# A two-direction delta-rule scan: outputs formed between the steps of its state, products emptied over two banks at once

## The chip, the cores and the metric

One core of a Trainium2 chip runs the whole kernel, a program of two transformer blocks. The metric is the time of one execution on the device in microseconds, the median of several runs. The change touches one function, a scan that runs four times.

## The reference

The part that matters is the RWKV-7 mixer of the first block, for eight heads of 64 columns, 512 tokens of the sequence (the latents) behind 256 tokens of context, forward and backward:

```
def rwkv7_scan(r, w, k, v, a, b, s0):
    def step(S, inp):
        r_t, w_t, k_t, v_t, a_t, b_t = inp
        sa = jnp.einsum('bhvk,bhk->bhv', S, a_t)
        S = S * w_t[:, :, None, :] + sa[..., None] * b_t[:, :, None, :] + v_t[..., None] * k_t[:, :, None, :]
        return S, jnp.einsum('bhvk,bhk->bhv', S, r_t)
    xs = tuple(jnp.moveaxis(t, 1, 0) for t in (r, w, k, v, a, b))
    S_fin, ys = lax.scan(step, s0, xs)
```

The context's final state is the latents' first one, and of the context no output is wanted. The outputs of both directions then go through a norm per head, a bonus and gates. Nothing of this is changed by the edit.

## The kernel before

`rwkv_scan` (from L1479) runs once for each pair of heads (`hp` 0 to 3). Head 0 of the pair stands on partitions 0 to 63, head 1 on 64 to 127. The 768 tokens are cut into `NB` = 12 chunks of `CH` = 64, of which the last `NL` = 8 are latents and the first `NBC` = 4 are context; the two directions `d` go through them in the orders of `order`.

The recurrence is brought into chunk form by a list of jobs, `pe_jobs`, each done for both directions. A job is one 64x64 product per chunk and head, 24 matmuls of fp32 data. The profile records each of these matmuls as two, so 48 records for one direction and 96 for both (L1583 in the helper `product`, L1588 in `turn`). SB, SM, SK and SR are the products of keys, decays and queries; KT, BT, AT and V turn inputs by the identity; T, M and N with their numbers are the rounds that invert the triangular system (solving rounds); XA, XV, ZA, ZV, YA and YV apply the inverse to the keys' side (A) and the values' side (V); G and H are the transition and the input of each chunk's state; RP is the state's factor in the latents' outputs. The jobs differ in how the matmuls lie on the array of 128x128: `four_tiles` goes round all four quarters of it, `both_heads` uses the two on the diagonal, one for each head.

Each job's result takes a region of PSUM of two banks, of which there are three; `region` gives them in turn. Half of the chunks lie in the first bank and half in the second, so that VectorE or ScalarE empties a region with two operations of 128x384 (G with four of 64x384), one after the other; the second one signals. `bank_free` makes a job of TensorE wait until the job three turns before it has been emptied. VectorE has the jobs of `dve_jobs` (masks, sums, L1772 to L1815), ScalarE those of `act_jobs` (copies, L1861), GpSimd multiplies by masks (L1905). ScalarE copies XV and ZV. Between these jobs each engine also does a share of the next pair's preparation (`prep`: among it `scale_rows` with L1310 and L1312, `carries` with L1319 to L1323, and `norm_keys`, L1296) and of the norm and gates of the pair before (`out`: `centre` L1390, `squares` L1376, `variance` L1396, `root` L1381 to L1384, `gates` L1370, `finish` L1406 to L1416). The order is written out by hand. `prep` is there for the first three scans, `out` for the last three.

Then come the ten steps of the state, S1 to S10: for each direction one matmul of a 128x128 by a 128x64 tile (L1700), and on VectorE one operation (L1815) that scales it and adds the chunk's input, giving the next state; S0 (L1780) is a copy. A step of a direction waits for VectorE's operation of the step before. All states are kept, one per chunk. Into the steps 1 to 4 and 7 to 10 TensorE puts a share of the modulation's products (`mods.rows_of`, L1443), from panels of 1 MB that stream in; they collect in a second bank of one region. When they are complete, ScalarE copies their rows (`keep`, L1452, four copies) into a part of the buffer of the outputs, and TensorE turns them into columns (`transpose`, L1460), which VectorE adds to a bias.

The outputs of the latents, job Y, come last: 16 cells for each direction, each the sum of three matmuls (L1706 values' part, L1707 direct part, L1708 state's part), 96 records per direction. Both directions are done in the order Y of direction 0, the modulation's transposes, Y of direction 1. ScalarE copies them out with two operations of 128x256 per direction (L1855). Then all engines meet (L1505), and after every second scan semaphores are cleared and they meet again (L3361).

Of the kernel before, what the change touches and what calls it, by code (L numbers as in the profile page):

```python
# [18 lines left out]
F32 = mybir.dt.float32  # L19
# [1459 lines left out]
def rwkv_scan(nc, g, hp, f, tri, prep_of, out_of):  # L1479
# [22 lines left out]
    dve_jobs = ["SB", "SM", "SK", "SR", "M1", "N1", "M2", "N2", "M3", "N3", "N4", "YA", "YV", "G", "H", "RP"] + ["S0"] + states  # L1502
    act_jobs = ["KT", "M0", "BT", "AKV", "T1", "T2", "T3", "T4", "AT", "XA", "XV", "ZA", "ZV", "Y"]

    with ExitStack() as tmp, nc.Block() as block:  # L1505
# [19 lines left out]
        bank = [[tmp.enter_context(nc.psum_tensor(f"{nm}q{r}{b}", [P, T], F32)) for b in range(2)] for r in range(3)]  # L1525
# [5 lines left out]
        turns += [(job, d) for job in pe_jobs[5:] for d in range(2)]  # L1531
        region = {turn: i % 3 for i, turn in enumerate(turns)}
        mods = ModPanels(nc, g, hp, f.Y[0:66, 1].rearrange("r (n c) -> r n c", c=P), bank[region["S1", 1]][1], prep_banks)
# [3 lines left out]
        cell = lambda d, name, h, i, n: bank[region[name, d]][i // n][head(h), (i % n) * CH:(i % n + 1) * CH]  # L1537
# [5 lines left out]
        halves = [slice(0, NB // 2), slice(NB // 2, NB)]  # L1543
        half_lat = [slice(0, NL // 2), slice(NL // 2, NL)]
# [31 lines left out]
        def _(pe):  # L1576
# [26 lines left out]
            def run(name, d):  # L1603
# [67 lines left out]
                elif name == "ZV":  # L1671
                    act(d, "XV")
# [4 lines left out]
                elif name == "YV":  # L1677
                    act(d, "ZV")
# [14 lines left out]
                elif name[0] == "S":  # L1693
                    n = int(name[1:])
                    dve(d, "H")
                    dve(d, f"S{n - 1}")
                    s = order[d][n]
                    if n == 1:
                        pe.wait_ge(zeroed, 2 + 2 * d)
                    last = mm(bank[region[name, d]][0][:, 0:HD], GT[d][:, s].rearrange("p h t -> p (h t)"), S[d][:, s], start=True, stop=True)  # L1700
# [8 lines left out]
                last.then_inc(pe_done[d], 1)  # L1709
# [13 lines left out]
            for job in pe_jobs[5:]:  # L1723
# [8 lines left out]
                if job == "Y":  # L1732
                    run(job, 0)
                    if out:
                        pe.wait_ge(out.step.sem, 7)
                    elif prep:
                        pe.wait_ge(prep.bonus_kept, 1)
                    mods.transpose(pe)
                    run(job, 1)
# [5 lines left out]
                elif out and job == "ZA":  # L1745
# [3 lines left out]
                elif job in states[0:4]:  # L1749
                    n = states.index(job)  # L1750
                    mods.rows_of(pe, 4 * n, 4 * n + 4)
                elif job in states[-4:]:
                    n = states[-4:].index(job) + 4
                    mods.rows_of(pe, 4 * n, 4 * n + 4)
# [8 lines left out]
        def _(dve):  # L1763
            V = nc.vector
            mask = lambda i, d, n: tri[:, i, d].unsqueeze(1).to_broadcast([P, n, CH])

            def run(name, d):
                own = lambda job: dve.wait_ge(dve_done[d], dve_jobs.index(job) + 1)
                if name == "SM":
                    dve.wait_ge(pe_done[d], pe_jobs.index(name) + 1)  # L1770
                    for b, c in enumerate(halves):
                        step.mark(V.tensor_tensor(MT[d][:, c], part(d, name, b), mask(2, d, NB // 2), ALU.mult))  # L1772
                    step.settle(dve)
                    two = tri[:, 8, 0].unsqueeze(1).to_broadcast([P, NB, CH])
                    V.tensor_tensor(MT[d], MT[d], two, ALU.add).then_inc(dve_done[d], 1)
# [7 lines left out]
                if name in ("SB", "SK"):  # L1783
                    for b, c in enumerate(halves):
                        last = V.tensor_tensor((AT if name == "SB" else AK)[d][:, c], part(d, name, b), mask(0, d, NB // 2), ALU.mult)  # L1785
                elif name == "SR":
                    for b, dst in enumerate((RB, RK)):
                        last = V.tensor_tensor(dst[d][:], part(d, name, b, NL), mask(1, d, NL), ALU.mult)
                elif name[0] in "MN":
# [3 lines left out]
                    for b, c in enumerate(halves):  # L1793
                        last = V.tensor_tensor(buf[d][:, c], buf[d][:, c], part(d, name, b), ALU.add)
                elif name in ("YA", "YV"):
                    buf = XA if name == "YA" else XV
                    for b, c in enumerate(halves):
                        last = V.tensor_tensor(buf[d][:, c], buf[d][:, c], part(d, name, b), ALU.add)
                elif name == "G":
                    two = tri[:, 8, 0].unsqueeze(1).to_broadcast([P, NB // 2, CH])  # L1800
                    for b, c in enumerate(halves):
                        for h in range(2):
                            last = V.tensor_tensor(GT[d][head(h), c, h], part(d, name, b)[head(h)], two[head(h)], ALU.add)
# [1860 lines left out]
```

## Time and profile before

| | us |
|---|---|
| median of 3 runs | 3119.36 |
| the three runs | 3119.67, 3111.02, 3119.36 |
| the profiled execution's own time | 3112.85 |
| its span, from first to last instruction | 3111.1 |
| TensorE busy | 2800.3 (90%) |
| VectorE, ScalarE, GpSimd busy | 1140.3, 939.6, 785.9 |
| mean granted clock of TensorE | 0.962 |
| the four scans begin with the products of SB | at about 408, 523, 642 and 758 |
| all four scans with their ends | 408 to 872 |

Times of rows are counted from the start of the span. "Busy" of TensorE is the union of its matmuls, whose ends are modelled. Idle time stands with the work after it, with what released it; "issue" is idle time in which the engine waited for nothing that the profile shows. The granted clock is a share of 2.4 GHz. The queue q8 carries instructions, not data.

### The profile page before, as it was taken

To read this page: it belongs to the slowest core of one execution; us is meant where nothing else is said; L and a number is where in the kernel's file an instruction comes from. 1 tells how busy PE (TensorE), PEld (TensorE's weight loads), DVE (VectorE), ACT (ScalarE), POOL (GpSimd) and SP (SyncE) were. 2 spreads that over 40 slices of the span, in tenths; PEclk is the share of its full clock that TensorE was granted. 3 is DMA by queue.
4 is the path that set the end of the run, shared out by engine and by line. 5 is a ranking of instruction groups with operands and counts; after the bars stand their busy time and mean duration, and the time that the engine had idled before them with its cause. 6 is when DMAs were issued, how large, how long until landed. Compare 5 with 4: busy or idle time off the path is not lost. (4 is left out here: it accounts for less than half of the span.)

```text
span 3111.1 us, 56253 instructions
## 1 busy us (share of the span) xinstructions
PE 2800.3 (90%) x25293; PEld 2160.5 (69%) x25293; DVE 1140.3 (37%) x1684; ACT 939.6 (30%) x1594; POOL 785.9 (25%) x218
## 2 busy tenths in 40 slices
PE   6987988888866988989899999988999999899998
PEld 4765877777754432333589989986888778678887
DVE  3434765665446000101454546463111113321111
ACT  3123233433322110110344555553222222132222
POOL 3320421231120000000132223221444434334442
PEclk8998999999987999999999999998999999999999
DMA  7111201012031899999422221321233322222221
GB/s 255 55 31 38 68 17 60 11 52 100 6 115 54 347 426 427 427 427 427 148 85 69 68 71 66 82 82 55 82 99 103 96 68 95 81 79 97 95 95 54
DMA packets 171635, 397.69 MB, mean 128 GB/s; under 512 B 9551, under 2 KB 99636, under 8 KB 146036
## 3 DMA queue, kind: packets, MB, share of 16 engines
q1 hardware_dynamic: 170416, 390.70, 34.3%
q8 instruction: 200, 3.28, 0.4%
q10 hardware_dynamic: 980, 3.40, 0.3%
q14 instruction: 39, 0.32, 0.0%
HBM read 387.71 MB, written 4.19 MB: 126 GB/s over the span
## 5 line engine op out<-in xcount | busy, mean ns | idle before, releaser
L179 POOL TENSOR_TENSOR weight_ring_lo<-weight_ring,weight_hi 128x2048 fp32r<-128x2048 f32 (+1 forms) x144 | 657.9, 4570 | 1986.9 <-ACT weight_hi L168 1947.7
L168 ACT CAST weight_hi<-weight_ring 128x2048 fp32r<-128x2048 f32 (+1 forms) x144 | 271.0, 1884 | 670.8 <-PE mlp_o L213 247.7
L213 PE MATMUL a_o<-weight_hi,latT_hi 128*128 128x512 f32 x576 | 176.7, 429 | 2.5 <-PEq L3361 2.5
L213 PE MATMUL a_o<-weight_ring_lo,latT_hi 128*128 128x512 f32 x576 | 158.2, 397 | 0.0
L213 PE MATMUL a_o<-weight_hi,latT_lo 128*128 128x512 f32 x576 | 157.8, 396 | 0.0
L1905 POOL TENSOR_TENSOR rws_E<-rws_AT,rw_tri 128x768 f32<-128x768 f32 x40 | 83.3, 2104 | 287.8 <-DVE rws_AT L1785 186.9
L213 PE MATMUL mlp_o<-weight_hi,mlp_hid_hi 128*128 128x512 f32 x512 | 138.8, 393 | 9.8 <-issue 9.8
L3237 DVE TENSOR_TENSOR x<-x,mlp_o 128x512 f32<-128x512 f32 x64 | 44.0, 687 | 281.4 <-PE mlp_o L213 281.4
L213 PEld LDWEIGHTS a_o<-weight_hi,latT_hi 128*128 128x128 f32 x576 | 132.9, 273 | 16.8 <-issue 8.2
L3222 DVE TENSOR_TENSOR mlp_hid<-mlp_hid,mlp_h 128x512 f32<-128x512 f32 x64 | 41.2, 685 | 272.7 <-ACT mlp_hid L3197 272.7
L213 PEld LDWEIGHTS a_o<-weight_ring_lo,latT_hi 128*128 128x128 f32 x576 | 134.2, 270 | 8.1
L213 PEld LDWEIGHTS a_o<-weight_hi,latT_lo 128*128 128x128 f32 x576 | 134.2, 270 | 7.9
L213 PE MATMUL mlp_o<-weight_ring_lo,mlp_hid_hi 128*128 128x512 f32 x512 | 138.4, 393 | 0.0
L213 PE MATMUL mlp_o<-weight_hi,mlp_hid_lo 128*128 128x512 f32 x512 | 137.1, 390 | 0.0
L204 PE MATMUL mlp_h<-latT_hi,weight_hi 128*128 128x512 f32 x512 | 129.3, 396 | 4.8 <-PEq L3361 4.8
L2441 ACT ACTIVATE moe_silu<-moe_t 128x256 f32<-128x256 f32 x32 | 12.3, 384 | 388.2 <-PE moe_t L2400 387.4
L204 PE MATMUL mlp_h<-latT_lo,weight_hi 128*128 128x512 f32 x512 | 128.3, 393 | 0.0
L204 PE MATMUL mlp_h<-latT_hi,weight_ring_lo 128*128 128x512 f32 x512 | 126.5, 389 | 0.0
L2384 PE MATMUL moe_gu<-weight_ring,moe_xsT 128*64 128x512 f32 x248 | 111.7, 596 | 12.9 <-DMA weight_ring<-in_w_up 7.3
L213 PEld LDWEIGHTS mlp_o<-weight_hi,mlp_hid_hi 128*128 128x128 f32 x512 | 96.9, 190 | 30.6 <-issue 10.5
L2385 PE MATMUL moe_gu<-weight_ring,moe_xsT 128*64 128x512 f32 x256 | 116.2, 598 | 0.0
L204 PEld LDWEIGHTS mlp_h<-latT_hi,weight_hi 128*128 128x128 f32 x512 | 97.6, 191 | 25.7 <-issue 5.4
(617 smaller groups left out, 5650.5 us busy)
## 6 DMA issues: line engine op xcount, KB each, us to landing
weight_ring<-in_mlp_w SPq DMA_DIRECT2D x64, 1024.0 KB, 5.2
weight_ring<-in_a_wqkv SPq DMA_DIRECT2D x36, 1024.0 KB, 5.0
weight_ring<-in_w_up SPq DMA_DIRECT2D x32, 1024.0 KB, 20.5
weight_ring<-in_w_gate SPq DMA_DIRECT2D x31, 1024.0 KB, 22.1
weight_ring<-in_w_down SPq DMA_DIRECT2D x31, 1024.0 KB, 20.8
weight_ring<-in_w_mod SPq DMA_DIRECT2D x24, 1024.0 KB, 5.8
weight_hi_spare<-in_w_up SPq DMA_DIRECT2D x12, 1024.0 KB, 20.0
weight_hi_spare<-in_w_gate SPq DMA_DIRECT2D x12, 1024.0 KB, 22.4
```

The source lines that it names most:

```text
L168: self.nc.scalar.copy(self.view(self.hi[:, q % 2], p, True), self.view(self.slots[self.slot[p]], p, True)).then_inc(self.hi_ready, 1)
L179: self.nc.gpsimd.tensor_tensor(self.view(self.lo[:, s], p, True), self.view(self.slots[s], p, True), self.view(self.hi[:, q % 2], p, True) ...
L204: last = nc.tensor.matmul(dst, left(a, k), right(b, k), start=(a + b + k == 0), stop=(a == 1 and k == KD - 1))
L213: last = nc.tensor.matmul(dst, left(a, HK * r + k), right(b, k), start=(r + a + b + k == 0), stop=(r == 1 and a == 1 and k == HK - 1))
L1905: nc.gpsimd.tensor_tensor(E[lv % 2][d][:], AT[d][:], tri[:, 2 + lv, d].unsqueeze(1).to_broadcast([P, NB, CH]), ALU.mult).then_inc(pool_don ...
L2384: x = nc.tensor.matmul(acc[e % 2][h][0:CAP, :], xsT[:, k, tokens], wg[:, r, cols(h)], start=(k == 0), stop=(k == KD - 1))
L2385: y = nc.tensor.matmul(acc[e % 2][h][CAP:P, :], xsT[:, k, tokens], wu[:, r, cols(h)], start=(k == 0), stop=(k == KD - 1))
L2441: nc.scalar.activation(silu[:, i], turn[i][:, :, 0:CAP], ACT.Silu).then_inc(silued, 1)
L3222: last = V.tensor_tensor(d, d, up[i % 2][h][:], ALU.mult)
L3237: last = V.tensor_tensor(d, d, acc[j][:], ALU.add)
```

## The change

It has three parts.

1. The job Y is gone as a block. After each state matmul for a latent chunk (steps 4 to 10) `outputs(n)` forms that step's outputs at once, for the chunk of each direction and both heads: 12 matmuls, 24 records, first the four values' parts, then the four direct ones, then the four states', in the order of the heads 0, 1, 1, 0. `outputs(11)` follows behind the last panel products. The results of each direction collect in one bank, `y_bank[d]`, the second bank of a region whose first is used by the states. The two directions' transposes of the modulation follow `outputs(11)`; ScalarE copies the outputs with one operation of 128x512 per direction, behind its copies of the panels' rows, and those rows are now put into `Kt`.
2. Every region is emptied by one operation over both banks (128x768, or [P, 2, 384] by its pattern; G by two of 64x768), on VectorE and ScalarE.
3. XV and ZV are copied by VectorE instead of ScalarE. With that, `scale_rows` and `carries` for the second direction move from behind N4 to behind ZV on VectorE, `centre` from behind N4 to behind XV, the sums of squares on TensorE from behind ZA to behind ZV, and on ScalarE `squares` and `root`, and what followed ZV (the zeroing of the other head's part of GT, and `keep`), to behind ZA.

```diff
-    dve_jobs = ["SB", "SM", "SK", "SR", "M1", "N1", "M2", "N2", "M3", "N3", "N4", "YA", "YV", "G", "H", "RP"] + ["S0"] + states
-    act_jobs = ["KT", "M0", "BT", "AKV", "T1", "T2", "T3", "T4", "AT", "XA", "XV", "ZA", "ZV", "Y"]
+    dve_jobs = ["SB", "SM", "SK", "SR", "M1", "N1", "M2", "N2", "M3", "N3", "N4", "XV", "ZV", "YA", "YV", "G", "H", "RP"] + ["S0"] + states
+    act_jobs = ["KT", "M0", "BT", "AKV", "T1", "T2", "T3", "T4", "AT", "XA", "ZA", "Y"]
...
-        bank = [[tmp.enter_context(nc.psum_tensor(f"{nm}q{r}{b}", [P, T], F32)) for b in range(2)] for r in range(3)]
+        bank = [tmp.enter_context(nc.psum_tensor(f"{nm}q{r}", [P, 2, T], F32)) for r in range(3)]
...
-        part = lambda d, name, b, n=NB // 2: bank[region[name, d]][b][:, 0:n * CH].rearrange("p (s t) -> p s t", t=CH)
+        part = lambda d, name, n=NB // 2: bank[region[name, d]][:, :, 0:n * CH].rearrange("p b (s t) -> p b s t", t=CH)
+        two_banks = lambda x: x.rearrange("p (b s) t -> p b s t", b=2)
+        y_bank = [bank[region[turn]][:, 1] for turn in (("S1", 0), ("S2", 0))]
...
-                elif name == "Y":
-                    dve(d, "RP")
-                    dve(d, states[-1])
-                    for h, s in both_heads(NL // 2):
-                        dst = cell(d, name, h, s, NL // 2)
-                        mm(dst, at(XV[d], *left(h, NBC + s)), RB[d][head(h), s], start=True, stop=False)
-                        mm(dst, Vt[head(h), NBC + s], RK[d][head(h), s], start=False, stop=False)
-                        last = mm(dst, S[d][head(h), NBC + s], Rp[d][head(h), s], start=False, stop=True)
+            def outputs(n):
+                for d in range(2):
+                    dve(d, "RP")
+                    dve(d, f"S{n - 1}")
+                quarters = [(h, d, order[d][n]) for h, d in ((0, 0), (1, 1), (1, 0), (0, 1))]
+                for h, d, s in quarters:
+                    mm(latent(d, h, s), at(XV[d], *left(h, s)), RB[d][head(h), s - NBC], start=True, stop=False)
+                for h, d, s in quarters:
+                    mm(latent(d, h, s), Vt[head(h), s], RK[d][head(h), s - NBC], start=False, stop=False)
+                last = {}
+                for h, d, s in quarters:
+                    last[d] = mm(latent(d, h, s), S[d][head(h), s], Rp[d][head(h), s - NBC], start=False, stop=True)
+                return last
...
                 if job == "Y":
-                    run(job, 0)
...
+                    last = outputs(NB - 1)
+                    for d in range(2):
+                        last[d].then_inc(pe_done[d], 1)
                     mods.transpose(pe)
-                    run(job, 1)
                     continue
...
-                elif out and job == "ZA":
+                elif out and job == "ZV":
                     out.square_sums(pe)
...
+                elif job in states:
+                    n = int(job[1:])
+                    if n >= NBC:
+                        outputs(n)
+                    if n <= 4:
+                        mods.rows_of(pe, 4 * n - 4, 4 * n)
+                    elif n >= 7:
+                        mods.rows_of(pe, 4 * n - 12, 4 * n - 8)
...
-                    for b, c in enumerate(halves):
-                        last = V.tensor_tensor(buf[d][:, c], buf[d][:, c], part(d, name, b), ALU.add)
+                    last = V.tensor_tensor(two_banks(buf[d][:, :]), two_banks(buf[d][:, :]), part(d, name), ALU.add)
+                elif name in ("XV", "ZV"):
+                    last = V.tensor_copy(two_banks((XV if name == "XV" else ZV)[d][:]), part(d, name))
...
-                elif prep and job == "N4":
+                elif prep and job == "ZV":
                     dve.wait_ge(pe_done[1], pe_jobs.index("BT") + 1)
                     prep.scale_rows(dve, 1)
                     prep.carries(dve, 1)
-                if out and job == "N4":
+                if out and job == "XV":
                     out.centre(dve)
...
-                if out and job == "XV":
+                if out and job == "ZA":
                     out.squares(act)
-                elif out and job == "ZV":
                     out.root(act)
-                if job == "ZV":
+                if job == "ZA":
```

## Rows read from the trace of the kernel before

**Rows 1.** Timeline of TensorE, second scan: start us, us, work [idle before <-releaser].

```profile
590.44 0.69 PE L1583 MATMUL rws_q<-rws_WV,weight_hi_spare 64*64 64x64 f32 x32 [1.85 <-issue]
...
594.22 0.27 PE L1583 MATMUL rws_q<-rws_AT,rws_E 64*64 64x64 f32 x1 [1.68 <-issue]
...
602.25 0.81 PE L1583 MATMUL rws_q<-rws_WV,weight_hi_spare 64*64 64x64 f32 x40 [1.79 <-issue]
...
636.11 0.41 PE L1460 MATMUL rws_p<-ident,rw_Y 2*128 2x2 f32 x8
```

**Rows 2.** The page: TensorE's busy time; the instruction queue (packets, MB).

```profile
PE 2800.3 (90%) x25293; PEld 2160.5 (69%) x25293; DVE 1140.3 (37%) x1684; ACT 939.6 (30%) x1594; POOL 785.9 (25%) x218
...
q8 instruction: 200, 3.28, 0.4%
```

**Rows 3.** Transfers from 655 to 732 us, third scan: the instruction queue.

```profile
q8 instruction: 21, 0.34, 1.9%
```

**Rows 4.** Third scan by stretch: PE, PEld, DVE, ACT, POOL busy, clock, DMA.

```profile
655.00:732.00 77.00, 67.54 (x2583) 58.85 (x2581) 53.22 (x84) 42.97 (x85) 19.85 (x10) 1.00 0.02 5
```

**Rows 5.** First state matmul to last copy, four scans, by stretch.

```profile
502.08:522.42 20.34, 17.94 (x496) 15.62 (x496) 5.48 (x23) 2.75 (x8) 0.00 (x0) 1.00 0.63 209
616.71:640.48 23.77, 21.86 (x496) 19.39 (x496) 9.99 (x29) 2.75 (x8) 0.00 (x0) 0.78 0.54 179
734.16:757.84 23.68, 21.49 (x496) 18.94 (x496) 10.47 (x31) 2.71 (x8) 0.00 (x0) 0.78 0.54 180
850.88:872.07 21.19, 17.97 (x496) 15.81 (x496) 9.76 (x30) 2.75 (x8) 0.00 (x0) 1.00 0.56 201
```

**Rows 6.** Timeline of TensorE, first scan, steps of the state.

```profile
502.08 0.64 PE L1700 MATMUL rws_q<-rws_E,weight_hi_spare 128*128 128x64 f32 x4 [1.15 <-DVE rws_E L1780]
502.65 0.63 PE L1443 MATMUL rws_q<-weight_ring,c_silu 128*2 128x64 f32 x32
503.20 0.66 PE L1700 MATMUL rws_q<-rws_E,weight_hi_spare 128*128 128x64 f32 x4
...
507.55 0.63 PE L1700 MATMUL rws_q<-rws_E,weight_hi_spare 128*128 128x64 f32 x4 [0.25 <-DVE rws_E L1815]
...
509.50 0.63 PE L1443 MATMUL rws_q<-weight_ring,c_silu 128*2 128x64 f32 x32 [0.45 <-DMA weight_ring<-in_w_mod]
```

**Rows 7.** Timeline of ScalarE, first scan, end of the stage.

```profile
514.45 1.49 ACT L1452 COPY rw_Y<-rws_q 2x256 f32<-2x256 f32 x4 [23.29 <-PE rws_q L1443]
517.72 0.65 ACT L1855 COPY rw_Y<-rws_q 128x256 f32<-128x256 f32 x2 [1.78 <-PE rws_q L1708]
```

**Rows 8.** By stretch: the second scan's last stage, cut where the clock changes.

```profile
616.71:624.80 8.09, 7.09 (x189) 5.91 (x189) 7.57 (x21) 0.00 (x0) 0.00 (x0) 1.00 0.57 191
624.80:635.00 10.20, 9.98 (x178) 8.90 (x176) 2.19 (x7) 1.45 (x4) 0.00 (x0) 0.50 0.74 246
635.00:640.48 5.48, 4.80 (x140) 4.58 (x136) 0.24 (x2) 1.29 (x4) 0.00 (x0) 1.00 0.11 38
```

**Rows 9.** By stretch: line L1688 alone, while H is formed, second scan.

```profile
607.70:613.70 6.00, 5.83 (x96) 5.66 (x96) 1.00 0.03 7
```

**Rows 10.** Groups by line and form, 400 to 880 us.

```profile
L1794 DVE TENSOR_TENSOR weight_hi_spare<-weight_hi_spare,rws_q 128x384 f32<-128x384 f32 x112 | 55.7, 548 | 51.3 <-PE rws_q L1583 51.0
...
L1775 DVE TENSOR_TENSOR weight_hi_spare<-weight_hi_spare,rw_tri 128x768 f32<-128x768 f32 x8 | 13.9, 1732 | 0.3
...
L1376 ACT ACTIVATE rw_rk<-rw_Y 128x512 f32<-128x512 f32 x6 | 3.6, 654 | 4.3 <-DVE rw_Y L1390 4.3
...
L1296 DVE TENSOR_TENSOR weight_ring<-weight_ring 128x768 f32<-128x768 f32 x3 | 2.8, 948 | 0.0
```

**Rows 11.** Timeline of VectorE, second scan, from N4 to YA.

```profile
586.51 2.49 DVE L1310 TENSOR_TENSOR rw_Bh<-weight_ring 128x768 f32<-128x768 f32 x1
...
590.00 1.28 DVE L1390 SCALAR_TENSOR_TENSOR rw_Y<-rws_p,rw_Y 128x512 f32<-128x512 f32 x2
599.00 1.95 DVE L1798 TENSOR_TENSOR rws_AT<-rws_AT,rws_q 128x384 f32<-128x384 f32 x4 [7.72 <-PE rws_q L1583]
```

More of the change, by code:

```diff
@@ L1764, in _ @@
             V = nc.vector
-            mask = lambda i, d, n: tri[:, i, d].unsqueeze(1).to_broadcast([P, n, CH])
+            mask = lambda i, d, n=NB // 2: tri[:, i, d].unsqueeze(1).unsqueeze(1).to_broadcast([P, 2, n, CH])
+            unit = lambda rows: tri[rows, 8, 0].unsqueeze(1).unsqueeze(1).to_broadcast([rows.stop - rows.start, 2, NB // 2, CH])
             def run(name, d):
@@ L1770, in run @@
                     dve.wait_ge(pe_done[d], pe_jobs.index(name) + 1)
-                    for b, c in enumerate(halves):
[L1772 to L1775, printed above, removed]
+                    step.link(dve, V.tensor_tensor(two_banks(MT[d]), part(d, name), mask(2, d), ALU.mult))
+                    V.tensor_tensor(two_banks(MT[d]), two_banks(MT[d]), unit(slice(0, P)), ALU.add).then_inc(dve_done[d], 1)
                     return
@@ L1783, in run @@
                 if name in ("SB", "SK"):
-                    for b, c in enumerate(halves):
-                        last = V.tensor_tensor((AT if name == "SB" else AK)[d][:, c], part(d, name, b), mask(0, d, NB // 2), ALU.mult)
+                    last = V.tensor_tensor(two_banks((AT if name == "SB" else AK)[d][:]), part(d, name), mask(0, d), ALU.mult)
                 elif name == "SR":
                     for b, dst in enumerate((RB, RK)):
-                        last = V.tensor_tensor(dst[d][:], part(d, name, b, NL), mask(1, d, NL), ALU.mult)
+                        last = V.tensor_tensor(dst[d][:], part(d, name, NL)[:, b], tri[:, 1, d].unsqueeze(1).to_broadcast([P, NL, CH]), ALU.mult)
                 elif name[0] in "MN":
@@ L1814, in run @@
                     s, s1 = order[d][n], order[d][n + 1]
-                    last = V.scalar_tensor_tensor(S[d][:, s1], bank[region[name, d]][0][:, 0:HD], f.carry[:, d, s:s + 1], H[d][:, s],
+                    last = V.scalar_tensor_tensor(S[d][:, s1], bank[region[name, d]][:, 0, 0:HD], f.carry[:, d, s:s + 1], H[d][:, s],
                                                   ALU.mult, ALU.add)
@@ L1853, in run @@
                 if name == "Y":
-                    for b, c in enumerate(half_lat):
-                        last = nc.scalar.copy(f.Y[:, d, c.start * CH:c.stop * CH].rearrange("p (s t) -> p s t", t=CH), part(d, name, b, NL // 2))
+                    last = nc.scalar.copy(f.Y[:, d], y_bank[d])
                 else:
@@ L1858, in run @@
                         act.wait_ge(pool_done[d], LV)
-                    dst = {"KT": Kt, "M0": M, "BT": Bt, "AKV": WV, "AT": At, "XA": XA, "XV": XV, "ZA": T1, "ZV": ZV}.get(name, T1)[d]
-                    for b, c in enumerate(halves):
-                        last = nc.scalar.copy(dst[:, c], part(d, name, b))
+                    dst = {"KT": Kt, "M0": M, "BT": Bt, "AKV": WV, "AT": At, "XA": XA}.get(name, T1)[d]
+                    last = nc.scalar.copy(two_banks(dst[:, :]), part(d, name))
                 last.then_inc(act_done[d], 1)
@@ L1868, in _ @@
             act.wait_ge(v_placed, 1)
-            for b, c in enumerate(halves):
-                last = nc.scalar.copy(Vt[:, c], part(0, "V", b))
-            last.then_inc(v_turned, 1)
+            nc.scalar.copy(two_banks(Vt[:]), part(0, "V")).then_inc(v_turned, 1)
             for job in act_jobs[1:]:
```

44 lines of the change are left out of this document (16 added, 28 removed).

## The prediction

> **What bounds the kernel now.** I read the page first: TensorE is busy 90% of the span, and the scan is only four stretches of it. So the question is what each stage of a scan waits for, and I went on with the stretches table, the transfers, and the engines' timelines.
>
> A scan has two stages that differ. In the long one (banks of products, solving rounds, G, H, RP) the timeline of TensorE in the second scan shows stops of 1.7 to 1.9 us released by "issue", in the middle of a product: no engine is awaited [rows 1]. The stops stand about 3.9 us apart. The instruction queue tells why. Over the span it brought 200 packets of 3.28 MB, 16.4 KB each, beside 25293 matmuls and as many weight loads, so a packet is some 126 matmuls with their loads [rows 2]. From 655 to 732 us it brought 21 packets, one per 3.85 us (77.0 over 20 intervals) [rows 3], while TensorE ran 2583 matmuls at full clock, one per 29.8 ns [rows 4]. That is the rate at which packets come, 3.85 us / 128 = 30.1 ns. The reader is to see that TensorE's work there goes at the pace of its instructions, whatever VectorE and ScalarE save.
>
> The short stage, S1 to the end of the block, has 496 matmuls in each scan and takes 20.34, 23.77, 23.68 and 21.19 us, 89.0 together [rows 5]. Its instructions would come in 496 / 128 x 3.85 = 14.9 us, so it is bound by something else: TensorE in order, with idle pieces between steps where the panels' products are absent (0.25 us and more) and before a panel's transfer (0.45) [rows 6]; then the Y products in one block at the end; then ScalarE's last copies [rows 7]. In the second scan, and likewise in the third (0.78 of full), the clock was granted at 0.50, the lower level of 1.2 GHz, for 10.20 us from 624.8 on, with TensorE busy 9.98 of them, after a stretch in which it was busy 7.09 of 8.09 us; it rose while the Y products ran [rows 8].
>
> **The sum's base** is the profiled execution: span 3111.1 us, own time 3112.85. The median of the three runs, 3119.36, lies 6.5 above it, the fastest run 1.8 below. I take the gain from the trace and subtract it from the median.
>
> **Part 1, outputs between the steps.** The work stays: 96 cells' matmuls (192 records) per scan. A pair of state matmuls takes 0.57 us (502.08 to 502.65), a step's share of the panels' products 0.55 (to 503.20) [rows 6]. The 96 Y records of one direction took 3.27 us, from the first copy of the panels' rows (514.45) to the copy of the first direction (517.72) [rows 7], 34 ns each. The new order never has three in a row on the same half of the array; H, which has two in a row, took 5.83 us for 192 (96 of L1688 and, alternating with them, as many of L1687) [rows 9], 30.4 ns each. I take H's, 24 x 30.4 = 0.73 us per step (bounds: Y's 0.82, and 0.52, were they at the pace of XV's 32 in 0.69 us [rows 1], which uses all four quarters of the array and not the two used here).
>
> TensorE then has 10 x 0.57 + 8 x 0.55 + 8 x 0.73 = 15.9 us with no idle piece: S5 and S6 get 0.73 us each to cover VectorE's step, and the panels have longer to land. The panels' products end at 15.2. What is late next is ScalarE: their rows' copies (1.49 us [rows 7]) now hold up the transposes, which lay behind 3.3 us of Y before, so TensorE stands from 15.9 to 16.8, then transposes for 0.4 [rows 1]. ScalarE's two Y copies follow the rows' at once, each 128x512 like an L1376 of 0.65 us [rows 10], about 0.6 apart: end at 18.1. Against it the stages lose 20.34 - 18.1 = 2.2, 5.7, 5.6 and 3.1, together 16.6 us. Of that, 10.2 us / 2 = 5.1 in each of two scans, 10.2 in all, is the lower clock. I expect it to stay full: the stretch that fell was the one with S5 and S6 nearly bare, and the Y products, which raised it again, are what now fills it.
>
> Added: two waits per step and direction pair on vector semaphores already passed (RP, and the S that the state matmul has awaited). Nothing is queued longer behind them; some 30 instructions are a quarter of a packet, under 1 us over a scan, and lie below the 14.9. With loads landing in the stage, the supply may falter in it; unseen in the first scan's Y, so between 0 and two stops of the size of [rows 1] per scan. I take 0.6 a scan, -2.4 us. The idle tail before the next block grows by about 1 us, and the clock may fall there: half of one scan's opening at the lower level, between 0 and 1.7 a scan; I take 1.2 once.
>
> **Part 2, two banks in one operation.** A pair of 128x384 from a bank is about 1.02 us on VectorE (548 ns each, overlapped); a 128x768 addition, alone, is 948 ns (L1296) [rows 10]. So 0.07 us per pair, on 32 pairs per scan on VectorE (G's four operations become two) and, for want of a nearer row, on ScalarE's 24 too: 56 x 0.07 = 3.9 us per scan of engine time. In the solving rounds nothing of it reaches the end: the 3.85 us per packet covers it. In the opening (SB, SM, SK) VectorE is the later one, and I take 0.15 per scan, 0.6 in all; bounds 0 and 15.7, were everything on the path. No row shows an operation over two banks. From below its cost is 0.95; from above 1.73, as the costliest 128x768 in the scan (L1775 [rows 10]). I take 0.95, because L1775 has all operands in SBUF, as L1310 with 2.49 us [rows 11], and both stand beside GpSimd's operations, while L1794, which reads PSUM as the merged ones do, averages 0.55 over 112.
>
> **Part 3, XV and ZV on VectorE.** Four copies of 0.95, added to VectorE, taken from ScalarE; the rescaling (from L1310 on, 3.5 us from 586.51 to the centring at 590.00) moves from behind N4 to behind ZV, and the squares and root of the head before behind ZA. Before, VectorE idled 7.72 us ahead of YA [rows 11]. Queued behind the moved 3.5 us are now YA, variance and YV; TensorE's second YV awaits YA's bank. ZV's 96 records at the pace of 590.44's 32 in 0.69 us end at 596.3, the copies at 597.3, the rescaling at 600.8, YA at 601.7: YV's second half would start then, and 602.25 is where the packet came anyway [rows 1]. Cost 0 under that cover; 3 us per scan in three scans without it.
>
> **Sum.** -16.6 - 0.6 + 2.4 + 1.2 = -13.6 us, nearly; I say -13.3, so 3119.4 - 13.3 = 3106.1 us (3099.6 in a run like the profiled one).
>
> **Rule against row.** The rows say that TensorE stops every 3.9 us for a packet. The Trainium skill (Runtime: NRT & Kernel Launch, Instruction fetch mechanics) says that the sequencer streams blocks of 16 KiB ahead and that crossing one is mostly hidden. The block size agrees with the 16.4 KB; "hidden" would make it rival 1.
>
> **The rivals.**
> 1. The stops are no pace but follow the products' hand-overs, so shorter copies shorten the rounds too. For it: copies do end just before some resumptions. Against: 3.85 us between packets over 77 us. Then part 2's 15.7 us come on top, less the 0.6 already taken: 3119.4 - 13.3 - 15.1 = 3091. Chance 0.08. The page's rule, by which the fetch hides, leads here.
> 2. The clock still falls in the short stage. For it: it did in two of four scans, with TensorE busy 88% before; the small matmuls remain. Against: the first and fourth scans kept it with the same work, and the bare steps are gone. 10.2 us are lost again: 3116. Chance 0.2.
> 3. The supply bounds the short stage once it is dense and transfers run: three stops of 1.2 us more per scan, 14 us less 2.4 taken: 3118. For it: 36 records per step with panels already come at 1.12 us, 31 ns each. Chance 0.12.
> 4. Slower: an operation over two banks, on three-level patterns, costs what L1775 does, 1.73. Then 0.71 us on 36 operations in each of four scans is 102 us of VectorE; TensorE and VectorE alternate in the rounds, so a third, 34 us, is on the path: 3119.4 - 13.3 + 34 = 3140. It decides from (13.3 + 9.4) / 48 = 0.47 us over the pair, 1.5 us per operation. Chance 0.05.
> 5. The change is smaller than told, for instance with the final copies as late as before: between no change and -5 us. Chance 0.05.
>
> **Numbers.** A measurement of this kernel tells about 0.3%, 9.4 us, from no change: faster is below 3110.0. The forecast has 0.50; its own spread (how much clock time there was in the other runs) puts it within the bound in about 1 of 8. Faster: 0.44 + 0.08 + a little of rival 2 = 0.56. Slower: 0.05. Same: 0.39. The range takes in the forecast, rivals 2 and 3 for their larger part, and half of rival 1: 3096 to 3117.
>
> **What would show it.** Right: S1 to the last Y copy 18 to 19 us in all four scans; the granted clock 1.00 in them; no long block of Y products; ScalarE's Y copies of 128x512 straight behind the panels' rows; TensorE waiting for those rows before the transposes. The long stage as long as before, one packet per 3.85 us, with the merged operations near 0.95 us. Wrong: a clock of 0.50 in the short stage (2), "issue" stops within it (3), merged operations above 1.5 us (4), a long stage shorter by over 2 us (1), or TensorE waiting for VectorE at YV or the gates (part 3).

## The result, and the profile after

The changed kernel takes 3105.64 us, the median of 8 runs (3102.09 to 3108.59); the kernel before, beside it, 3119.31 (8 runs, 3110.23 to 3123.63). The ratio is 0.9961, 95% interval 0.9947 to 0.9974. That is 13.7 us less, where 13.3 were forecast. By the interval anything from 8 to 17 us less fits, and a second measurement of the same two kernels on another chip, reported below, has 10.1 us. The profiled execution took 3103.15 us, its span is 3101.3.

The page of the changed kernel: busy times, and the queue that carries instructions.

```profile
PE 2795.1 (90%) x25293; PEld 2156.4 (70%) x25293; DVE 1143.5 (37%) x1572; ACT 920.3 (30%) x1462; POOL 785.4 (25%) x218
...
q8 instruction: 201, 3.29, 0.4%
```

Against [rows 2] nothing large has moved: the same 25293 matmuls, 244 operations fewer on VectorE and ScalarE together, and ScalarE 19 us less busy. None of that says where 13.7 us come from. The stages do. The four short stages of the changed kernel, from the first state matmul to the last copy of the outputs (columns as in [rows 5]):

```profile
505.36:524.32 18.96, 17.57 (x496) 15.27 (x496) 5.48 (x23) 2.52 (x6) 0.00 (x0) 1.00 0.59 189
616.96:637.06 20.10, 17.61 (x496) 15.27 (x496) 10.10 (x29) 2.52 (x6) 0.00 (x0) 1.00 0.56 178
731.93:750.90 18.97, 17.57 (x496) 15.28 (x496) 10.38 (x31) 2.52 (x6) 0.00 (x0) 1.00 0.60 190
843.56:862.60 19.04, 17.64 (x496) 15.34 (x496) 10.32 (x30) 2.52 (x6) 0.00 (x0) 1.00 0.60 189
```

They take 77.1 us together, 11.8 less than the 88.9 between the same two events before (89.0 in the prediction, by windows cut a few hundredths wider), and the granted clock is 1.00 in all four, where two of [rows 5] have 0.78. The four long stages sum to 371.6 us, against 373.3. From the first SB product to the end of the fourth short stage it is 450.6 us, 13.4 less; ahead of the scans, where nothing was changed, the changed kernel's execution was 4.0 us later (SB at 412.0, not 408.0), and the tail is 0.3 shorter: 9.8 by the spans. The 4.0 us are chance: over all profiled executions of this document SB begins between 406.1 and 412.6 us, whatever the kernel.

TensorE's timeline in the first short stage, with one line of the second scan's at the end (start us, us, work, idle before and its releaser):

```profile
508.78 0.66 PE L1700 MATMUL rws_q<-rws_E,weight_hi_spare 128*128 128x64 f32 x4
509.37 0.45 PE L1714 MATMUL rws_q<-rws_RB,rws_E 64*64 64x64 f32 x8
509.65 0.40 PE L1716 MATMUL rws_q<-weight_hi_spare,rws_Vt 64*64 64x64 f32 x8
509.88 0.40 PE L1719 MATMUL rws_q<-rws_WV,rws_E 64*64 64x64 f32 x8
510.21 0.63 PE L1443 MATMUL rws_q<-weight_ring,c_silu 128*2 128x64 f32 x32
...
512.20 0.66 PE L1700 MATMUL rws_q<-rws_E,weight_hi_spare 128*128 128x64 f32 x4
...
513.64 0.66 PE L1700 MATMUL rws_q<-rws_E,weight_hi_spare 128*128 128x64 f32 x4
...
523.28 0.41 PE L1460 MATMUL rws_p<-ident,rws_Kt 2*128 2x2 f32 x8 [0.76 <-ACT rws_Kt L1452]
...
626.40 0.63 PE L1700 MATMUL rws_q<-rws_E,weight_hi_spare 128*128 128x64 f32 x4 [1.09 <-issue]
```

The outputs of a step are the three groups of eight between 509.37 and 510.21, 0.84 us. No step waits for VectorE any more, the bare ones S5 and S6 included (512.20 to 513.64, 1.44 us, no idle piece). One stop by "issue" stands in the second scan, and makes its 20.10.

ScalarE's timeline at the end of the same stage:

```profile
521.74 1.49 ACT L1452 COPY rws_Kt<-rws_q 2x256 f32<-2x256 f32 x4 [27.04 <-PE rws_q L1443]
523.25 1.07 ACT L1861 COPY rw_Y<-rws_q 128x512 f32<-128x512 f32 x2
```

The rows' copies release the transposes at 523.28, and the two outputs' copies, back to back behind them, set the end.

The merged operations, groups by line and form from 405 to 870 us (xcount, busy us, mean ns, idle before):

```profile
L1804 DVE TENSOR_TENSOR weight_hi_spare<-weight_hi_spare,rws_q 128x768 f32<-128x768 f32 x56 | 52.1, 951 | 54.3 <-PE rws_q L1583 54.3
...
L1866 ACT COPY rws_AK<-rws_q 128x768 f32<-128x768 f32 x40 | 30.6, 800 | 79.5 <-PE rws_q L1583 79.3
```

And the instruction queue in the long stage of the second scan, 532 to 609 us:

```profile
q8 instruction: 20, 0.33, 1.7%
```

The first of these packets comes at 533.40 us and the last at 607.73, so the 19 intervals between them are 3.91 us each, near the 3.85 of [rows 3].

### The profile page after: what moved, and what is told of

Read it like the earlier page. It is cut to its first block and busy times, and to the rows that moved or that the text cites. A ratio compares the mean times of both kernels' runs of the same rounds, so it can differ in the third digit from the quotient of the medians.

```text
span 3101.3 us, 56077 instructions
## 1 busy us (share of the span) xinstructions
PE 2795.1 (90%) x25293; PEld 2156.4 (70%) x25293; DVE 1143.5 (37%) x1572; ACT 920.3 (30%) x1462; POOL 785.4 (25%) x218
```

## The experiments

The theory: the gain is part 1's alone, and within it mostly the granted clock; parts 2 and 3 give nothing, because the supply of instructions paces the solving rounds. The rival: shorter hand-overs between the engines give part of it. The first four kernels ran on one chip beside 35 runs of the kernel before (3121.69 us), the others on two more chips. A ratio is always to the kernel before on the same chip.

**Part 1 alone.** The kernel before with `outputs(n)` between the steps, and the old two-operation copies everywhere else.

```diff
+                    if n >= NBC:
+                        outputs(n)
...
-                    for b, c in enumerate(half_lat):
-                        last = nc.scalar.copy(f.Y[:, d, c.start * CH:c.stop * CH].rearrange("p (s t) -> p s t", t=CH), part(d, name, b, NL // 2))
+                    last = nc.scalar.copy(f.Y[:, d], y_bank[d][:])
```

> The kernel before with part 1 alone: outputs between the steps, halves still emptied one after the other, XV and ZV on ScalarE. My theory (the long stage goes at the pace of the instruction packets, the short one loses its idle pieces and the lower clock): nearly the whole gain, 10 to 14 us faster than before; short stages of 19 to 20 us each, all at clock 1.00. Rival (the merged operations bring the gain): 0 to 5 us faster.

Measured: 3110.66 us, ratio 0.9965 (0.9951 to 0.9980). All that the change gives, within the interval. One expectation failed: in this kernel's second scan the clock did fall (below).

**Part 2 alone.** The changed kernel with job Y as a block again and XV, ZV on ScalarE: only the merged operations are left. Of the difference to the kernel before, one place:

```diff
-                        last = V.tensor_tensor(buf[d][:, c], buf[d][:, c], part(d, name, b), ALU.add)
+                    last = V.tensor_tensor(two_banks(buf[d][:, :]), two_banks(buf[d][:, :]), part(d, name), ALU.add)
```

> The kernel before with part 2 alone: one operation over two banks everywhere, Y as one block at the end. My theory: 0 to 3 us faster, the long stages within 1 us of before (94.0, 92.4 and 92.7 us in the scans 1, 3 and 4), merged additions near 0.95 us. Rival (shorter operations shorten the rounds): 8 to 15 us faster.

Measured: 3120.03 us, ratio 0.9991 (0.9975 to 1.0007). Nothing that can be told from zero. The merged additions take 951 ns here too. The long stages were to stay within 1 us of before; those of the third and fourth scan are 95.8 and 96.3 us long, 3.3 and 3.6 more, with the clock at 0.96 and 0.95 where the kernel before had 0.98 and 1.00.

**Parts 2 and 3.** The changed kernel with job Y as a block again.

```diff
+                    run(job, 0)
...
-                    last = outputs(NB - 1)
-                    for d in range(2):
-                        last[d].then_inc(pe_done[d], 1)
                     mods.transpose(pe)
+                    run(job, 1)
```

> The changed kernel with part 1 undone: parts 2 and 3, Y as one block. My theory: 0 to 3 us faster than before, as with part 2 alone, with part 3 worth nothing either way; the short stages again 20.3 to 23.8 us, some with the clock at 0.50. Rival (VectorE's copies of XV and ZV hold TensorE up): slower than part 2 alone by 3 us and more. Rival (they free ScalarE and so help): faster than part 2 alone by 3 us and more.

Measured: 3120.83 us, ratio 0.9997 (0.9981 to 1.0012). Nothing of part 3 can be told from zero either, and an effect of some 5 us could hide in the interval.

**The place or the order?** The changed kernel with its own outputs, in their new order and banks, all behind S10.

```diff
-                    last = outputs(NB - 1)
+                    for n in range(NBC, NB):
+                        last = outputs(n)
...
-                    if n >= NBC:
-                        outputs(n)
```

> The changed kernel with all eight steps' outputs formed after the tenth step, in the new order of the quarters, and not between the steps. If placement brings the gain (my theory): short stages of 19.5 to 20.5 us where the clock holds and 22.5 to 24 where it falls, 4 to 11 us slower than the changed kernel. If the new order of the quarters brings it: as fast as the changed kernel within 3 us. The 192 records in one block also tell what one costs without the changes between the array's shapes: 30 ns as in H, or 35 as between the steps.

Measured: 3119.14 us, ratio 0.9996 (0.9983 to 1.0009), 8.5 us more than part 1 alone on the same chip. The whole gain is gone, so it is the place. Its first and its fourth short stage, and two stops of TensorE in the fourth:

```profile
503.94:526.76 22.82, 21.07 (x496) 18.61 (x496) 5.67 (x23) 2.53 (x6) 0.00 (x0) 0.78 0.57 187
```

```profile
859.80:879.57 19.77, 17.16 (x496) 14.99 (x496) 9.81 (x30) 2.53 (x6) 0.00 (x0) 1.00 0.64 215
```

```profile
871.71 0.50 PE L1443 MATMUL rws_q<-weight_ring,c_silu 128*2 128x64 f32 x18 [0.90 <-issue]
...
875.68 0.39 PE L1716 MATMUL rws_q<-weight_hi_spare,rws_Vt 64*64 64x64 f32 x6 [0.24 <-issue]
```

At full clock the block at the end costs only 0.8 us against the 19.0 of the changed kernel, and 1.14 us of this stage are stops by "issue": without them it would be 18.6, no longer than the changed kernel's. The other 3.05 us of the first come with the clock at 0.78. So in this stage the place as such gains nothing; it pays where the steps would wait, or the clock would fall.

The block also answers what a record costs where the shape of the matmuls does not change. At full clock, in the first scan:

```profile
522.45 0.40 PE L1719 MATMUL rws_q<-rws_WV,rws_E 64*64 64x64 f32 x8
522.68 0.40 PE L1714 MATMUL rws_q<-rws_RB,rws_E 64*64 64x64 f32 x8
```

Eight records take 0.23 us, 29 ns each, and 24 take 0.70, where they take 0.84 between the steps.

**The block at the end, but no bare steps.** The changed kernel forms all outputs once more behind S10 (the result is the same). If it is something in the steps that lets the clock fall, and not the block, it must hold here although the block is back.

```diff
-                    last = outputs(NB - 1)
+                    for n in range(NBC, NB):
+                        last = outputs(n)
```

> The changed kernel with its latent outputs formed between the steps and then, all of them, once more after the last step (the result is the same): 7 sets of 24 products more after the states, about 0.71 us each at 29.6 ns. It has the block of outputs at the end, as the kernel before and the one with the outputs last, but the steps are filled. Theory that the bare steps are what lets the clock fall in the short stage: all four short stages at clock 1.00, 23.5 to 24.3 us each (19.0 + 5.0), about +20 us in all against the changed kernel. Theory that it is the block of outputs at the end, or chance: the clock falls in two or three of the four, 26 to 29 us in those, +30 us or more in all.

Measured: 3127.02 us, beside 3118.45 for the kernel before, ratio 1.0034 (1.0019 to 1.0048); 19.3 more than the changed kernel's 3107.76 in its own second measurement, on another chip. Two of its short stages, the first and the third:

```profile
506.90:531.89 24.99, 22.93 (x664) 20.47 (x664) 5.49 (x23) 2.52 (x6) 0.00 (x0) 1.00 0.53 171
```

```profile
743.84:770.09 26.25, 23.34 (x664) 20.53 (x664) 10.43 (x31) 2.52 (x6) 0.00 (x0) 1.00 0.50 163
```

All four are at 1.00. They last 25.0, 23.2, 26.2 and 25.4 us, where I expected 23.5 to 24.3: one is shorter, three are longer, and that is not the clock. TensorE's timeline has "issue" stops of 1.34 us in the first, none in the second, 1.99 in the third and 1.62 in the fourth, most of what these three are longer than the second. The two of the third stage:

```profile
761.32 0.28 PE L1443 MATMUL rws_q<-weight_ring,c_silu 128*2 128x64 f32 x5 [0.83 <-issue]
...
766.43 0.27 PE L1719 MATMUL rws_q<-rws_WV,rws_E 64*64 64x64 f32 x2 [1.16 <-issue]
```

Over all profiled executions: in the four kernels whose steps 5 and 6 stand bare (the kernel before, part 2, parts 2 and 3, outputs last) the mean clock of the short stage lay below 0.95 in 11 of 16 scans; in the nine with outputs between (36 scans) in one. That one is in the kernel with part 1 alone, second scan:

```profile
614.82:639.75 24.93, 23.52 (x496) 20.51 (x496) 10.44 (x29) 2.53 (x6) 0.00 (x0) 0.73 0.45 144
```

There the clock fell 1.9 us after S1, in steps that the change leaves as they were. So the fill makes a fall rare, not impossible.

The bare steps are not all that the fill takes away. Behind them TensorE also waits for the next panel, and the 16 scans differ in that. From the kernel before, the third scan and the fourth:

```profile
742.55 1.04 PE L1443 MATMUL rws_q<-weight_ring,c_silu 128*2 128x64 f32 x32 [0.81 <-DMA weight_ring<-in_w_mod]
```

```profile
857.46 0.63 PE L1700 MATMUL rws_q<-rws_E,weight_hi_spare 128*128 128x64 f32 x4 [0.45 <-DVE rws_E L1815]
858.02 0.63 PE L1443 MATMUL rws_q<-weight_ring,c_silu 128*2 128x64 f32 x32
```

The four fourth scans have the same two waits for VectorE in S5 and S6 and none for a panel, and all four keep the full clock. The other twelve wait for a panel as well, at least 0.28 us, and in eleven the clock falls. In the 36 filled scans TensorE waits for neither. So bare steps alone did not bring a fall here; whether the panel's wait is what adds it isn't shown, for in the third scan of the kernel before the clock fell at 740.85, ahead of that wait, and no run filled one of the two and left the other.

**The changed kernel again**, on the chip of three of the next kernels (ballast with two copies, products twice, rows first).

> The changed kernel once more, on the chip of the three that follow, so that they are compared with it and not across chips. Both theories: about 3105 us, 13 to 15 us under the kernel before.

Measured: 3107.76 us (12 runs) beside 3117.88 (26 runs), ratio 0.9965 (0.9951 to 0.9978): 10.1 us less, where I expected 13 to 15. Each run also has its mean clock over the whole execution: 0.9623 on average, 0.9583 for the kernel before. Among the 26 runs of the kernel before alone, a run is 2.06 us shorter for each 0.001 of clock (correlation -0.80); among the 35 and the 12 on the other chips it is 1.88 and 2.56. By these slopes the difference of 0.0040 is 7.5 to 10 us, of 10.9 between the two means.

The stages give a second estimate. In the first scan the kernel before kept its clock and took 20.34 us; with part 2 alone it spent 10.24 us at the lower level:

```profile
499.23:522.63 23.40, 21.90 (x496) 19.36 (x496) 5.67 (x23) 2.62 (x6) 0.00 (x0) 0.78 0.56 182
```

That is 3.1 us for such a fall (23.51, so 3.2, with parts 2 and 3), and two of them are 6 of the 11.8 us that the short stages lost in the profiled pair; the first and fourth stages, which kept the clock before, lost 1.4 and 2.1 each. So the clock is about half of the gain by the stages of the profiled pair, and three quarters or so by the slopes. Both are estimates: no run held the clock and moved the outputs.

**More work for VectorE in the rounds.** `ballast`, linked copies of 128x192 ahead of each sum of M1 to M3 and N1 to N3, which nobody reads; two copies first.

```diff
+                    if lv < 4:
+                        for _ in range(2):
+                            step.link(dve, V.tensor_copy(ballast[:], tri[:, 0:3, d]))
```

> The changed kernel with some 24 more VectorE copies of 128x192 a scan, two chained ahead of each sum of the solving rounds (their result is read by nothing); 5 to 9 us more of VectorE's work a scan. My theory, that the pace of TensorE's instructions sets the solving rounds and the hand-overs between engines fit beneath it: the long stages (about 93 us each) grow by 0 to 2 us, the kernel by 5 us at most. Rival, that the hand-overs set the rounds, which is why shorter copies should have paid: +3 to +6 us a scan, +10 to +25 us in all.

Measured: 3116.15 us, 8.4 more than the changed kernel beside it, between the two theories. So two more doses were run on another chip, one copy and four.

```diff
-                        for _ in range(2):
+                        for _ in range(1):
```

> The changed kernel with one VectorE copy ahead of each sum of the solving rounds, 15 us of VectorE's work in all. Slack under the packets: the first 15 us fit, +0 to +3 us against the changed kernel. A fixed share of 28%: +4 us. Hand-overs set the rounds throughout: +8 to +15.

Measured: 3105.97 us, ratio 0.9965 (0.9954 to 0.9976), the same ratio as the changed kernel without any.

```diff
-                        for _ in range(2):
+                        for _ in range(4):
```

> The changed kernel with four chained VectorE copies ahead of each sum of the solving rounds, where the kernel with two had +8.4 us by its medians (between both theories, so neither is told by it). If instruction packets and hand-overs share the rounds, and slack under the packets is used up by the first copies: VectorE gets 60 us more in all, twice those of two, and now nearly all of the second 30 us shows: +25 to +40 us against the changed kernel. If a fixed part of VectorE's work always shows (28% of it, 8.4 of 30): +17 us. If the growth of two was noise and packets hide it all: under +10.

Measured: 3144.18 us, ratio 1.0090 (1.0073 to 1.0106). VectorE's busy time in all grew by 14, 30 and 54 us (1144.5 to 1158.5, 1174.5, 1198.7); the time by -1.8, +8.4 and +36.4 (the first and the last across two chips, on which the kernel before differs by 0.6). The first dose costs nothing and the last most of itself, so it is no fixed share. How sharp the turn is isn't clean: the long stages grew by 10.4 us with two copies and 35.7 with four, but they also spent some 8 and 41 us more at the lower clock, which can be up to half of that time, 4 and 20 us. The waits of TensorE in the long stage of the third scan show it turn from one limit to the other. Without ballast (waited for: us in total, times, longest):

```profile
PE rws_q L1583 <- issue: 8.5, 10, 1.8
...
PE rws_q L1583 <- DVE weight_hi_spare L1804: 0.5, 1, 0.5
```

With two copies:

```profile
PE rws_q L1584 <- issue: 6.3, 5, 2.1
PE rws_q L1584 <- DVE weight_hi_spare L1808: 5.7, 6, 1.8
```

With four:

```profile
PE rws_q L1584 <- DVE weight_hi_spare L1808: 10.6, 10, 1.9
PE rws_q L1584 <- issue: 3.7, 3, 1.8
```

The supply is the limit, and the hand-over from VectorE lies close beneath it: 14 us in all (3.5 a scan) fit into the slack, 30 don't.

What shows the supply is where the stops stand, and not how far apart the packets are. In this stage of the changed kernel's second measurement the stops by "issue" of more than 0.25 us from 676.02 us on come 127, 127, 253, 380 and 127 matmul records after one another, multiples of a packet's 127, whichever product TensorE is in. The interval between packets only follows their use: with four copies 23 packets came in the same stage, one per 4.43 us.

**More instructions for TensorE.** The products M1, N1 and M2 twice in the same place.

```diff
+                cells = list(cells)
-                for h, s in cells:
+                for h, s in cells * (2 if name in ("M1", "N1", "M2") else 1):
```

> The changed kernel with the products M1, N1 and M2 formed twice over in the same place (the result is the same): 144 more 64x64 products with their weight loads, 288 records a scan. Theory that the delivery of instructions paces this stage (one stop and one packet of 256 instructions to some 127 matmuls with their loads, 3.85 us each): 576 instructions, 2.25 packets, +8.7 us a scan, +35 us in all. Theory that the array's own time does: 288 records by 16.3 ns, +4.7 us a scan, +19 us in all. Theory that the hand-overs between engines set the rounds and TensorE has idle time to spare: under +10 us in all.

Measured: 3139.06 us, 31.3 more than the changed kernel, ratio to the kernel before 1.0074 (1.0058 to 1.0090). The packets' pace had said 35, the array 19, spare time under 10. Over 4 x 288 records that is 27 ns each. Its instruction queue brought nine packets more, the 2.25 a scan worked out:

```profile
q8 instruction: 210, 3.44, 0.4%
```

The four long stages sum to 412.7 us against 376.4 in the changed kernel beside it, 9.1 us per scan for 288 records, 31.5 ns each; this profiled execution is the slowest of the six, 9.1 us above their median. The same stage of the third scan in both, doubled first:

```profile
655.80:759.92 104.12, 87.71 (x3247) 77.19 (x3247) 65.55 (x76) 41.00 (x57) 28.29 (x14) 0.98 0.03 7
```

```profile
632.22:727.16 94.94, 81.55 (x2958) 71.18 (x2959) 65.44 (x76) 40.72 (x57) 28.51 (x14) 0.98 0.03 8
```

9.18 us more for 289 more records, with the same operations on the other engines and the same clock. I take this to be the term that hides part 2: a stage that waits for instructions gains nothing from shorter copies.

**The last copy of the rows covered.** From step 7 on the panels' products stand ahead of the outputs.

```diff
-                    if n >= NBC:
-                        outputs(n)
                     if n <= 4:
                         mods.rows_of(pe, 4 * n - 4, 4 * n)
                     elif n >= 7:
                         mods.rows_of(pe, 4 * n - 12, 4 * n - 8)
+                    if n >= NBC:
+                        outputs(n)
```

> The changed kernel with one order turned round: from step 7 on the panels' rows copies stand ahead of the latent outputs on TensorE, so that the last of these copies on ScalarE is covered by outputs instead of holding TensorE for 0.76 us ahead of the transposes. Theory that the end of the short stage is set by this copy: 19.0 us to 18.3 us, 0.7 us a scan, about -2.8 us in all against the changed kernel. Rival, that TensorE's stream or the last Y copy sets the end: no difference (within 1 us).

Measured: 3105.10 us, ratio 0.9967 (0.9955 to 0.9979), 2.7 below the changed kernel beside it; the two ratios can't be told apart. Its first short stage and the end of it:

```profile
502.87:520.99 18.12, 17.42 (x496) 15.19 (x496) 5.49 (x23) 2.52 (x6) 0.00 (x0) 1.00 0.61 199
```

```profile
519.94 0.41 PE L1460 MATMUL rws_p<-ident,rws_Kt 2*128 2x2 f32 x8
```

The wait of 0.76 us ahead of the transposes is gone, and the stage is 0.84 shorter; the others took 21.1 (two stops by "issue", 1.00 and 1.74), 18.6 and 19.2 (one, 0.71). The mechanism is as expected; that the kernel is faster for it isn't shown.

## Why the prediction was right, point by point

**The short stage, 18.1 forecast, 19.0 measured.** The term that was mis-sized is a step's outputs. I took 24 records at H's 30.4 ns, 0.73 us; they take 0.84. The eight records of each family start 0.28, 0.23 and 0.33 us apart: the middle one is at 29 ns a record, and the other two have 0.05 and 0.10 us more, at the changes from and to matmuls on the whole array. H is a long run of quarter products and has no such changes, so its row could not show them; nor has the block with the outputs last, which takes 0.70 for 24. With seven sets ahead of the rows' copies that is most of what moved the panels' end from 15.2 to 16.4 us after S1. The remainder of the end was right: TensorE waits 0.76 us (0.9 forecast) for the rows' copies, and ScalarE's output copies end 1.09 us behind it (1.3). Over four scans the miss is 0.9 x 4 = 3.6 us.

**Supply in the short stage, 2.4 us forecast.** One stop of 1.09 us in four scans; none in the second execution of the changed kernel on another chip, three of 1.00, 1.74 and 0.71 with the rows first. For the changed kernel the term was at least twice too large, and the scans without a stop at 18.97 show that the stream itself isn't bound by it. The waits that it had beside it are an eighth of a packet of 256 instructions, not a quarter; nothing rests on that.

**The clock, rival 2.** It held in all four scans, as forecast. The reason given, that the bare steps let it fall and the Y products raise it, is half shown. The experiment with the block back behind filled steps kept the clock in all four scans, so the block isn't the cause; the fourth scans, bare and at full clock, speak against the bare steps alone. The prediction counted that the panels have longer to land, but not that the end of those waits could be what keeps the clock. The price was too high too. It took half of 10.2 us for a fall, 5.1; the first scans show 3.1, because the idle pieces between the steps shrink when the matmuls take longer (2.40 us of idle time in the stage at full clock, 1.50 in the other). The short stage's sum doesn't use that split, but rival 2's 10.2 us do.

**How the total came so near.** In part by luck. The short stages gave 11.8 us, where 16.6 - 2.4 = 14.2 were forecast. The 1.2 us for the tail were not paid, 0.6 for part 2 isn't seen, and the long stages were 1.7 us shorter for no reason that a run shows. So the scans of the profiled pair differ by 13.4. Of that the two executions keep 9.7, for the 4.0 us ahead of the scans. The medians differ by 13.7, and by 10.1 on the other chip: the forecast of 13.3 is inside what was measured, but that it lies 0.4 us from the first result says nothing. The profiled execution of the kernel before lay 6.5 us under its median, which I named and didn't explain. Its mean clock of 0.962 was high for its kernel, whose runs average 0.958; by the slope of 2.06 that is 7 to 8 us, so it is the likely reason.

**The tail, 1.2 us.** The clock fell to the lower level behind the short stage in three scans, 3.4 us each, but two such pieces stand in the kernel before too, and the long stages behind them aren't longer; no cost of it is seen.

**Part 2, +0.6 us, and rival 4.** The merged addition takes 951 ns, the 0.95 taken from L1296; rival 4's 1.73 is out. No gain of it reaches the time: 0.9991 (0.9975 to 1.0007) alone. ScalarE's merged copy, for which I had no row, takes 800 ns.

**Part 3, 0.** Not contradicted: 0.9997 for parts 2 and 3 together, beside 0.9991 for part 2. The cover is there, but it is thin: the ballast shows 3.5 us a scan of VectorE's time as free in the solving rounds, and 7.5 as costing 2.

**Rival 1, and the rule.** The long stages are 371.6 us, 1.7 less (the changed kernel's second execution has 376.4, so 1.7 is nothing). Rival 1's 15 us are not there, and the doubled products pay 27 to 32 ns per matmul record, about the packets' pace. The prediction took the even interval of packets as its proof; as the ballast shows, that interval would look even under any limit, and the stops at each 127th record are the better sign. The Trainium skill (Runtime: NRT & Kernel Launch, Instruction fetch mechanics) has the crossing of a block mostly hidden; here the trace disagrees wherever 64x64 products follow each other: TensorE stands 8.5 us in ten stops in one long stage. I gave the rival 0.08; its "for", that copies end just ahead of some resumptions, was a true sign of the second limit close by.

**Rival 3** needed three stops a scan and had one in four scans. **Rival 5** fell with the timeline: every piece of the change is where it was said to be.

## What to carry to other kernels

Where a serial chain leaves TensorE with thin matmuls and short gaps, move independent products into its steps. They cover two things at once, the wait for the other engine and the wait for the next load: in the scans that had kept the full clock that gave 1.4 and 2.1 us here, and half of the gain or more came from a clock that no longer fell. Compare the mean clock of the profiled execution with that of the other runs before taking its falls as typical, and price a fall by a stage with it against the same stage without, not by half its length. Before shortening VectorE's and ScalarE's operations, look whether TensorE's waits say "issue" at even distances in records; if they do, the slack of the other engines can be measured with ballast in doses. That fewer matmul instructions would shorten such a stage follows from the doubled products, but no run here formed fewer.

## What the runs showed of the hardware

- TensorE stops for its instructions in long runs of small matmuls: stops by "issue" of 0.2 to 2.1 us, the longer ones mostly 127 records or a multiple apart, one packet of 16.4 KB per 3.9 us or so, and 27 ns (medians) to 32 ns (third scan, traces) for each further 64x64 matmul record with its load.
- A change between products on quarters of the array and matmuls on all of it costs 0.05 to 0.10 us beyond the records' pace (0.84 us for 24 records between the steps, 0.70 for 24 in the block at the end).
- One VectorE addition of 128x768 over two PSUM banks takes 951 ns, one ScalarE copy 800 ns.
- Whether the clock falls differs between executions of one program, and the mean clock of a run goes with most of the spread between runs (1.9 to 2.6 us per 0.001). In the short stage it fell in 11 of 12 scans with bare steps and a wait for a panel, in 0 of 4 with bare steps alone, and in 1 of 36 with neither; what on the chip decides it in a given scan is open.
- 10.24 us at the lower level made a stage with idle pieces 3.1 us longer (20.34 to 23.40), not 5.1; 13.65 us made a dense one 6.0 us longer (18.97 to 24.93).
